# Scaling the token mixers' output rows of the first half: in-place multiplies and transposes in place of products with diagonal matrices

## What is computed

```python
y = _rms(jnp.stack([ya, yb, yc, yd], axis=2)).reshape(bsz, seq, D_MIX) * mix_out_g[l]
x = x + g1 * (y @ w_out[l])
h = rms_norm(x, norm2_g[l]) * (1.0 + sc2) + sh2
x = x + g2 * conv_glu(h, ffn_w_up[l], ffn_conv_w[l], ffn_conv_b[l], ffn_w_down[l])
```

## Time and profile before

| what | value |
|---|---|
| three runs, us | 1284.63, 1287.73, 1289.82 (median 1287.73) |
| profiled execution, us | 1285.75 |
| its span in the profile, us | 1283.7 |
| mean granted TensorE clock, share of full speed | 0.987 |
| PE busy | 1206.8 us, 94% of the span, 5708 instructions |
| DVE busy | 718.8 us, 56%, 1405 instructions |
| ACT busy | 577.2 us, 45%, 993 instructions |
| POOL busy | 630.3 us, 49%, 317 instructions |

### The profile page before, as it was taken

The page is one execution under the profiler, slowest core; times in us unless marked ns, Lnnn a source line. Parts: engine busy times, 40 slices in busy tenths (PEclk is TensorE's granted clock), DMA queues, the critical chain, the costliest instruction groups (busy, mean ns, idle before and its releaser), DMA issues.

```text
span 1283.7 us, 17073 instructions
## 1 busy us (share of the span) xinstructions
PE 1206.8 (94%) x5708; PEld 993.3 (77%) x5708; DVE 718.8 (56%) x1405; ACT 577.2 (45%) x993; POOL 630.3 (49%) x317
## 2 busy tenths in 40 slices
PE   2898999987899899999999999989999999999997
PEld 1687778866788788888878887878788888888876
DVE  6943877888966898989984344353621112211224
ACT  4236656545852444224422666553444234422443
POOL 1135566783405255445545566325255445544554
PEclk9999999998999999999999999999999999999999
DMA  8457753451122122232224443424222222222223
GB/s 315 155 184 258 204 160 132 149 152 33 50 82 98 50 99 98 98 114 94 89 96 148 139 139 114 145 76 142 70 96 97 98 99 98 98 97 91 93 102 141
DMA packets 58568, 153.91 MB, mean 120 GB/s; under 512 B 6505, under 2 KB 20201, under 8 KB 58513
## 3 DMA queue, kind: packets, MB, share of 16 engines
q1 hardware_dynamic: 47472, 135.12, 31.3%
q10 hardware_dynamic: 11040, 18.09, 4.3%
HBM read 142.66 MB, written 10.52 MB: 119 GB/s over the span
## 4 chain that ended last, share of the span: by engine, by line
PE 40%; issue 24%; POOL 15%; DVE 11%; DMA 4%; ACT 4%; ACTq 1%; POOLq 0%; SPq 0%; DVEq 0%
PE ps L1858 10%; POOL w_lo L559 10%; PE ps L1859 9%; PE ps L1861 9%; DVE unread L1332 4%; POOL act_lo L712 3%; PE ps L2145 2%; POOL w_ada L598 1%; PE ps L1839 1%; PE ps L1840 1%; PE ps L1842 1%; PE ps L2124 1%; PE ps L2134 1%; DMA w_ada<-in_w_ada 1%; DVE h_lo L1290 1%
## 5 line engine op out<-in xcount | busy, mean ns | idle before, releaser
L559 POOL TENSOR_TENSOR w_lo<-w_raw,w_hi 128x1024 fp32r<-128x1024 f32 x148 | 356.5, 2409 | 435.9 <-ACT w_hi L724 435.9
L1858 PE MATMUL ps<-h_hi,w_hi 128*128 128x512 f32 x896 | 355.8, 397 | 4.5 <-POOL w_lo L565 4.5
L1859 PE MATMUL ps<-h_lo,w_hi 128*128 128x512 f32 x896 | 350.7, 391 | 0.0
L1861 PE MATMUL ps<-h_hi,w_lo 128*128 128x512 f32 x896 | 331.9, 391 | 0.0
L724 ACT ACTIVATE w_hi<-w_raw 128x1024 fp32r<-128x1024 f32 x148 | 156.8, 1059 | 334.0 <-PE ps L1861 327.4
L1858 PEld LDWEIGHTS ps<-h_hi,w_hi 128*128 128x128 f32 x896 | 169.2, 189 | 40.3 <-POOL w_lo L565 5.7
L1861 PEld LDWEIGHTS ps<-h_hi,w_lo 128*128 128x128 f32 x896 | 168.9, 188 | 36.1
L1859 PEld LDWEIGHTS ps<-h_lo,w_hi 128*128 128x128 f32 x896 | 169.4, 189 | 32.5
L1732 DVE SCALAR_TENSOR_TENSOR ps<-conv_in,conv_w,ps 128x512 f32<-128x512 f32 x44 | 33.2, 753 | 206.4 <-ACT ps L1133 206.4
L1858 PE MATMUL ps<-act_hi,w_hi 128*128 128x512 f32 x352 | 140.3, 399 | 5.0 <-POOL act_lo L712 2.6
L1861 PE MATMUL ps<-act_hi,w_lo 128*128 128x512 f32 x352 | 137.4, 390 | 0.0
(11 more groups left out here) (252 smaller groups left out, 1849.6 us busy)
## 6 DMA issues: line engine op xcount, KB each, us to landing
w_raw<-in_w SPq DMA_DIRECT2D x173, 512.0 KB, 3.2
w_ada<-in_w_ada SPq DMA_DIRECT2D x48, 512.0 KB, 4.1
x_sb<-in_x SPq DMA_DIRECT2D x4, 1024.0 KB, 9.8
q_st<-qk_dram SPq DMA_DIRECT2D x32, 128.0 KB, 4.1
out<-fin_o ACTq DMA_DIRECT2D x16, 256.0 KB, 2.1
qi_st<-qi_dram ACTq DMA_DIRECT2D x18, 128.0 KB, 4.3
qk_dram<-qk_hi ACTq DMA_DIRECT2D x4, 512.0 KB, 3.0
qk_dram<-qk_lo ACTq DMA_DIRECT2D x4, 512.0 KB, 3.9
```

What stands on the lines that cost most here:

```text
L559: pool.tensor_tensor(r(w_lo[:, slot]), w_raw[:, slot], w_hi[:, slot], ALU.subtract).then_inc(w_lo_ready, 1)
L1858: pe.matmul(ps[:, bank], r(hi_t[:, kk]), r(xh(kk)), start=(i == 0), stop=False)
L1859: pe.matmul(ps[:, bank], r(hi_t[:, kk]), r(xl(kk)), start=False, stop=False)
L1861: mm = pe.matmul(ps[:, bank], r(lo_t[:, kk]), r(xh(kk)), start=False, stop=last_k)
```

## The change

For h = 0 the diagonals go. `y_scales` multiplies the rows of each mixer, four blocks of 256 columns (128x1024), in place by the inverse roots, the form that `scale_late_rows` uses for h = 1, and signals `y_scaled` instead of `y_diag_ready`. TensorE turns the rows with plain transposes in both halves. The count of `y_scaled` for h = 1 begins four higher. `diag_y` and its semaphore are gone; nothing else is put in its memory.

```diff
-        diag_y = at("diag_y", [P, 4, HB, P], RB + 4096)
...
-        y_diag_ready = sem("y_diag_ready")
...
                     for m_ in groups:
-                        dve.tensor_tensor(diag_y[:, m_], ident[:].unsqueeze(1).to_broadcast([P, HB, P]),
-                                          y_scale[:, 4 * m_:4 * m_ + 4].unsqueeze(2).to_broadcast([P, HB, P]),
-                                          ALU.mult).then_inc(y_diag_ready, 1)
+                        rows = y[:, 0:HB, W * Y_GROUPS[m_]:W * Y_GROUPS[m_] + W]
+                        dve.tensor_tensor(rows, rows, y_scale[:, 4 * m_:4 * m_ + 4].unsqueeze(2).to_broadcast([P, HB, W]),
+                                          ALU.mult).then_inc(y_scaled, 1)
...
                     if h == 0:
-                        pe.wait_ge(y_diag_ready, i // 2 + 1)
+                        pe.wait_ge(y_scaled, i // 2 + 1)
                     elif i < 4:
-                        pe.wait_ge(y_scaled, i // 2 + 1)
+                        pe.wait_ge(y_scaled, HB + i // 2 + 1)
                     else:
                         pe.wait_ge(y_scaled_act, i // 2 - 1)
...
-                        if h == 0:
-                            tr = pe.matmul(at_, rows, diag_y[:, i // 2, t], start=True, stop=True)
-                        else:
-                            tr = pe.transpose(at_, rows, ident[:])
+                        tr = pe.transpose(at_, rows, ident[:])
```

## The result

The changed kernel is a little slower: a median of 1290.43 us in 11 runs (1287.48 to 1293.31) against 1287.02 in 11 runs of the kernel before, a ratio of 1.0028 with a 95% interval of 1.0016 to 1.0040, or +3.6 us (2.1 to 5.2). Run again in a later series it gave 1.0023 (1.0008 to 1.0037), +3.0 us. The forecast was +0.8 us, no change by the bound of 0.5%. Of the runs of the kernel before in the later series, four of 1311 to 4258 us are left out of every ratio and average.

The account below looks back on a forecast made before the run. The bound was when h = 0's output projection starts: y_lo's delay, past its 1.26 us slack, moves it +0.82 us despite shorter TensorE work. Mean 1287.0 + 0.8 gave 1287.8 us, range 1284.2 to 1291.3.

Parts of the forecast that it names:

- What bounds: Start of h = 0's output projection: its first product decides the time; y_lo had 1.26 us of slack behind TensorE.
- VectorE's part: DVE in h = 0: four diagonals become four 128x1024 multiplies, 1.21 us each, 1.12 in the queue against 0.60.
- The round trip through ACT: Between third and fourth multiplies: early_out, ACT's square and root, then DVE's inversion; keeps its 1.74 us.
- The rival of POOL holding the DVE: DVE multiplies in h = 0 held by POOL, each costing 2.06 us; +4.6 us, 1291.6; chance 0.03.
- TensorE's part: TensorE in h = 0: products of 0.92 us per tile become transposes of 0.65; 2.2 us won if TensorE bound.
- Where the two meet: Ahead of the projection: TensorE waits 1.2 and 1.45 us; first product at 373.55 instead of 372.73, +0.82 us.
- The clock: Behind the transposes: clock at 1.2 GHz level for three us costs 1.5 us; +2.3 in all, 1289.3; chance 0.17.
- the signs that the prediction had named against itself: In the changed profile: multiplies near 0.7 us, first product before 372.7, or clock of 0.5 behind the transposes.
- the likeliest case: Whole kernel: the forecast of +0.4 to +1.3 us, given 0.61.
- second case: The falling clock behind the transposes: +2.3 us in all, 1289.3; chance 0.17.
- The sentence of the Trainium skill on transposes and the clock: TensorE: transposes do not count as busy for the clock as products do; the prediction found the trace disagreeing.
- The rule of the Trainium skill on the DVE and GpSimd: A two-SBUF-input VectorE instruction contends with a GpSimd instruction reading SBUF; the loser waits for the whole of it.

Follow-up runs that it names:

- the run with three tiles: Changed kernel, with TensorE entering the output projection when three y_lo tiles are ready, not four; ratio 1.0003 (0.9984 to 1.0023).
- without the loop: Changed kernel with the loop of the first output projection written out as eight units; ratio 1.0010 (0.9991 to 1.0029).
- both variants with transposes whose first wait was 1.8: Changed kernel entering the projection at three y_lo tiles, ratio 1.0003; changed kernel with the first projection's loop written out, ratio 1.0010.
- the two kernels that filled them: Changed kernel with fp32 identity products replacing first-half transposes, ratio 1.0007; changed kernel with 10 and 8 idle transposes in the waits, ratio 1.0007.
- products and a long wait: Kernel before, diagonal products kept, with three idle DVE multiplies ahead of y_lo; ratio 1.0029 (1.0016 to 1.0043).
- the transposes alone: Kernel before, diagonals still built but unread, first-half rows turned unscaled by transposes; ratio 0.9993 (0.9980 to 1.0005).
- products and waits: Changed kernel with identity products instead of first-half transposes, plus two idle DVE multiplies ahead of the fourth mixer's inversion; ratio 1.0026 (1.0009 to 1.0042).
- the mixed version: Changed kernel with ACT scaling mixer D's rows, earlier first y_hi and y_lo, three-tile entry, and diagonals kept for the fourth mixer; ratio 0.9988 (0.9974 to 1.0003).

## Why the prediction was right in its way and short in its size

*What bounds.* Right for the part that the change moves: the question was when the projection starts, and `y_lo` ends last (the run with three tiles moved the start by its pitch, 0.66 us).

*VectorE's part.* Right: the four multiplies last 1.22 us each (1.21 taken), and POOL was idle beside them. `y_lo` starts at 6.56 us after the inversion against 4.43 before, +2.13 where +2.08 was worked out. The round trip through ACT kept its length: 1.55 us from `early_out`'s write of `y` to the fourth multiply (371.15 to 372.70), 1.54 before (366.44 to 367.98). The rival of POOL holding the DVE did not occur.

*TensorE's part.* Mis-sized: I took 0.65 us for a tile of four transposes, the larger of the two values from the second half. Two tiles take 1.06 us here, 0.53 each. As TensorE was not the bound this did not move the start, but it lengthened the first wait from the worked-out 1.2 to 1.83 us.

*Where the two meet.* Mis-sized: from the end of the fourth `y_lo` to the first product I took 0.16 us from a transpose in straight code. Here the wait stands ahead of a loop; it measured 0.45, and 0.05 without the loop. With the 0.05 us by which `y_lo` came later than worked out, this makes +0.82 into +1.16, and with the shorter transposes the second wait 1.87 instead of 1.45.

*The clock.* This is the step that failed: the forecast put the cost of the clock at nothing. I gave the fall 0.17, at +2.3 us, because the second half has "the same pattern" at a clock of 1.00. It has not. There, waits of 1.64 and 1.55 us have 2.4 us of transposes between them; here they are longer, 1.83 and 1.87, partly through the two errors above, and 1.06 us of work lies between. The second half held its clock in and behind that step in 13 of the 14 profiles of the study; the changed step lost it in both profiles, and in both variants with transposes whose first wait was 1.8. A clock of 0.5 behind the transposes was also one of the signs that the prediction had named against itself. That the difference lies in the waits is supported by the two kernels that filled them; why one execution loses the clock and another does not is open. The forecast was thus the likeliest case of a list whose second case happened, with the term that I did have (1.5 us, measured 1.7).

*What was drawn on beside the rows.* The sentence of the Trainium skill on transposes and the clock ("TensorE: Matmul & The Clock Gate", section "Part 4: PE-mode transpose") pointed in the right direction, but not for its reason: with the waits filled by more transposes the clock stayed at 1.00, and with products and a long wait it fell once. The rule of the Trainium skill on the DVE and GpSimd ("SBUF — State Buffer", section "Who interferes with whom") was not called upon, since no POOL instruction ran beside the multiplies; they took 1.22 us, against the 2.149 of the earlier trace rows beside POOL.

The expectations of the experiments missed as well: the wait of the transposes alone (1.87 for 0.9), the fall with products and waits, which did not come, and the second wait there (0.92 for 1.2).

## What to carry to other kernels

Before making an engine's work cheaper, work out what it will then wait for: here 3 us of TensorE work went, the DVE's chain ahead of the next stage grew by 2.1, and all that was won came back as waits, at exactly the place where the back-to-back products start. Such waits can have a second price on TensorE, the clock: it fell in seven of the nine profiles with a wait of over 1.8 us ahead of this projection, and in none of the five without. When comparing with a stretch that keeps its clock, compare the lengths of the waits and the work between them, not just their number. Where all engines wait for one short instruction, as here for the scaling of the fourth mixer, keep the cheap form for that one, and move other work off its engine to one that idles; the mixed version did this and started the projection 1.66 us earlier than the kernel before.

## What the runs showed of the hardware

Products with the identity, which take TensorE longer than transposes (0.92 against 0.53 us for a tile of four), left the start of the projection where it was, since nothing waited for TensorE there, and in the profile the clock held. The ratios are 1.0007 and 1.0023 in the same series, with intervals that overlap.

Every fall around this step but one has the same size, a shortfall of 1.70 to 1.71 us; the one without the loop had 3.41. The times of one and the same kernel go with its clock. Of 89 timed runs of the kernel before, the 37 with a mean granted clock of 0.988 or more average 1284.8 us, and the 20 with 0.983 or less 1288.9. So single runs of this kernel can't tell effects under 4 us, while the distance from the inversion to the first product repeats to 0.02 us (9.73 in three profiles and 9.74 in a fourth; 10.75 and 10.73 in two of one kernel).

A wait ahead of this loop on TensorE cost 0.4 us more than the same wait with the loop written out, when it was really waited for (0.45 us from the last `y_lo` needed to the first product, against 0.05 in the one profile without the loop).
